# Index scores earlier, two feature tiles in the attention loop, query blocks in reverse order

## The chip, the cores and the metric

One core of one Trainium2 chip runs the whole program. The time is the device time of one execution in microseconds; the figure that counts is the median of the runs. The names in the profile are PE (TensorE matmuls), PEld (its weight loads), DVE (VectorE), ACT (ScalarE), POOL (GpSimd) and SP (SyncE, which issues most DMAs).

## The reference

The reference is one inference step of two decoder layers on 512 prompt tokens and 8 samples, width 1024. Each layer normalises x, multiplies it by one input projection, and feeds four token mixers from column groups of the result; their outputs go through one output projection, and a gated feed-forward part follows. The mixer that the change touches is A, sparse attention: 8 indexer heads score every earlier key, each query keeps the best 128 (64 for a sample), and 4 heads of 64 attend over the kept keys.

```python
def select_keys(qi, wi, ki, qpos, topk):
    s = jnp.einsum('bqhd,bsd->bqhs', qi, ki) * IDX_DIM ** -0.5
    score = jnp.einsum('bqhs,bqh->bqs', jax.nn.relu(s), wi * N_IDX_HEADS ** -0.5)
    score = jnp.where(kpos[None, None, :] <= qpos[None, :, None], score, -jnp.inf)
    _, idx = lax.top_k(score, topk)
    return idx, idx <= qpos[None, :, None]
```

B is a short gated convolution, C a convolution of 31 taps with a layer norm, D a state-space scan with its own convolution of 4 taps.

## The kernel before, in words

Every engine runs one program written out in order by hand; semaphores join them, and `past(layer, sem, value)` is the count to wait for in a layer. [...] All of float32 accuracy is made of three products: a value is split into a rounded part (`hi`, cast on ScalarE) and the rest (`lo`, a subtraction), and hi*hi, hi*lo and lo*hi are summed in PSUM.

A layer of the kernel has these stages up to the output projection:

1. **Token tiles.** The queries, keys, values and indexer columns are made with tokens on the partitions, in 15 tiles `(s, t)`: slab s of three (0 indexer, 1 queries and half the keys, 2 the other half and the values), and t of four blocks of 128 tokens and the samples (t = 4, `QT`). `slab_upper` on ScalarE and `slab_lower` split the weight slabs: slab 0 on VectorE (`first_slab_lower`, L1731), slabs 1 and 2 on GpSimd (L2527). Tiles of slab 0 for t < 4 are made together (L729 to L743), the others one after another (L745 to L770). ScalarE copies each out (`tok_ready`).
2. **Index scores.** After tile (1,0), TensorE waits for VectorE's rotary (`rope_done` 2), transposes the indexer queries and keys (`turn`, L767 to L769), and issues 24 index products (3 query blocks by 8 heads, `IDX`), four at a time at half tiles from (1,1) to (1,4) (`IDX_PLACES`). ScalarE rectifies each (`idx_rectified`), VectorE weights and adds it (L1823 to L1832), with four PSUM banks and two buffers in SBUF between them.
3. **Top-k.** VectorE alone: the mask of future keys, the rotary of the queries (L1837), then 16 rounds of the eight largest and their replacement over three blocks (L1840 to L1851). In round 4 it turns aside for the rotary of the keys and the samples (L1841 to L1844), whose end (`rope_done` 5) GpSimd waits for before it stores k and goes on with its subtractions.
4. **Feature tiles.** Meanwhile TensorE makes the remaining columns with features on the partitions, in 18 tiles of 48 products (`feature_products`, L774). SP loads a weight tile, ScalarE casts it (`tile_upper`), GpSimd subtracts (`tile_lower`), and ScalarE copies the result out (`feature_out`, which casts the weights of the tile after next first, L1335). Tiles 0 to 6 come first (`SPREAD_FROM` = 7), then 24 products between each of 8 samples' spread rows (L811 to L813), on which VectorE computes the samples' scores (L1860 to L1877): 11 tiles up to the loop (`LOOP_TILES`).
5. **The attention loop** (L931 on TensorE, L1410 on ScalarE, L2099 on VectorE) has 16 steps, one per query block and head, in `STEPS` order, block 0 first. Per step VectorE masks the logits (L2107), ScalarE takes the exponential, VectorE scales (L2120), TensorE transposes the probabilities (L965), ScalarE copies them, and TensorE multiplies by the values, for two heads at once (L954); logits are made in pairs (L924). A block b has (b + 1) * 128 keys, so the size of all of these goes with the block. Between them VectorE does the samples' attention, the gates and the convolution of D, and from step 11 the rows of the samples' states (`state_rows`, L2053, which waits for TensorE's `turn_state_rows`) and the states; TensorE does `STEP_PRODUCTS[j]` feature products twice in each of steps 0 to 10, and from step 12 the taps of the long convolution (`conv_c_group`, L912). Up to tile 11 two pairs of banks alternate (`tile_bank`); later tiles have one pair, so that tile i waits until tile i - 1 has been copied out (L780). `tiles_ending` tells ScalarE in which half step a tile ends.
6. Then the scan of D, the last two feature tiles and the output projection follow.

```python
SPREAD_FROM = 7
STEP_PRODUCTS = (14, 12, 13, 9, 13, 9, 13, 9, 13, 9, 9)
LOOP_TILES = SPREAD_FROM + NS * PER_SPREAD // PER_TILE
```

Of the kernel before, what the change touches and what calls it, by code (L numbers as in the profile page):

```python
# [22 lines left out]
F32 = mybir.dt.float32  # L23
# [94 lines left out]
def hybrid_decoder(nc, d, out):  # L118
# [24 lines left out]
    with ctx:  # L143
# [220 lines left out]
        first_lo = x8_turned  # L364
        per_layer[first_lo.num] = 2
        slab_hi, slab_lo = sem("slab_hi", 5), sem("slab_lo", 3)
# [77 lines left out]
        SPREAD_FROM = 7  # L444
# [3 lines left out]
        STEP_PRODUCTS = (14, 12, 13, 9, 13, 9, 13, 9, 13, 9, 9)  # L448
# [23 lines left out]
        STEPS = [(blk, h) for blk in range(QT) for h in range(HEADS)]  # L472
        IDX = [(blk, h) for blk in range(1, QT) for h in range(IH)]
        IDX_PLACES = [(1, 1, 1), (1, 2, 0), (1, 2, 1), (1, 3, 0), (1, 3, 1), (1, 4, 0)]
        IDX_AT = {place: range(4 * i, 4 * i + 4) for i, place in enumerate(IDX_PLACES)}

        def tok_bank(g):

            return 2 + g % 2 if g > QT else 7 if g == QT else 2 + g
# [20 lines left out]
        with nc.Block() as block:  # L500
# [126 lines left out]
            def _(pe):  # L627
# [23 lines left out]
                for layer in range(DEPTH):  # L651
# [58 lines left out]
                    g = 0  # L710
                    for s in range(N_TOK):
                        if s == 1:
# [16 lines left out]
                        if s == 0:  # L729
                            starts = [a for a, _, _, _ in tok_pieces[0]]  # L730
                            for k in range(KC):
                                pe.wait_ge(*past(layer, m_lo_ready, k + 1))
                                if k in starts:
                                    pe.wait_ge(*past(layer, first_lo, starts.index(k) + 2))
                                hi, lo = tok_k_of(tw_hi, 0, k), tok_k_of(tw_lo, 0, k)
                                for t in range(QT):
                                    to = bank(tok_bank(t))[:, 0:tok_w[0]]
                                    u_k, lo_k = u_hi[:, k, t * P:(t + 1) * P], m_lo[k][:, t * P:(t + 1) * P]
                                    pe.matmul(to, u_k, hi, start=(k == 0), stop=False)  # L739
                                    pe.matmul(to, u_k, lo, start=False, stop=False)  # L740
                                    last = pe.matmul(to, lo_k, hi, start=False, stop=(k == KC - 1))  # L741
                                    if k == KC - 1:
                                        last.then_inc(tok_summed, 1)  # L743
                            g = QT
                        for t in range(QT if s == 0 else 0, QT + 1):  # L745
                            m = P if t < QT else NS
                            to = bank(tok_bank(g))[0:m, 0:tok_w[s]]
                            if g > QT:
                                pe.wait_ge(*past(layer, tok_ready, g - 1))
                            for k in range(KC):  # L750
                                if s and t == 0 and k in [a for a, _, _, _ in tok_pieces[s]]:
                                    pe.wait_ge(*past(layer, slab_lo, sum(len(p) for p in tok_pieces[1:s]) +
                                               [a for a, _, _, _ in tok_pieces[s]].index(k) + 1))
                                u_k, lo_k = u_hi[:, k, t * P:t * P + m], m_lo[k][:, t * P:t * P + m]
# [4 lines left out]
                                if k == KC // 2 - 1:  # L759
                                    idx_products((s, t, 0))  # L760
# [170 lines left out]
                    for j in range(-1, len(STEPS) + 2):  # L931
# [13 lines left out]
                        if j >= 3 and j % 2:  # L945
                            blk, h = STEPS[j - 3]
                            pe.wait_ge(*past(layer, prob_t_ready, j - 1))
                            if h == 0 and blk >= 1:
                                pe.wait_ge(*past(layer, mixed_out, blk))
# [1683 lines left out]
```

## Time and profile before

| | us |
|---|---|
| Median of 3 runs | 1466.51 |
| Lowest, highest | 1465.22, 1470.06 |
| Profiled execution | 1465.05 |
| Its span, first to last instruction | 1463.3 |
| Busy PE, DVE, ACT, POOL | 1368.9, 1017.8, 652.4, 184.2 |
| Mean granted TensorE clock | 0.964 |

A window row gives the stretch in us from the start of the span, its length, the busy time of PE, PEld, DVE, ACT and POOL with the count of instructions, the granted TensorE clock (1.00 is 2.4 GHz, 0.50 is 1.2 GHz), the DMA share and GB/s. A timeline row gives start, duration, engine, line, operation, output and inputs by name, partitions and elements, and the count merged into the row; in square brackets stands how long the engine was idle before it and whose instruction released it. Durations of merged rows are those of the whole group.

### The profile page before, as it was taken

Reading aid. Unit: us, or ns where it says so; the run is one execution under the profiler, and the core shown is the slowest. Engines: PE = TensorE matmul, PEld = TensorE weight load, DVE = VectorE, ACT = ScalarE, POOL = GpSimd, SP = SyncE. Lnnn points to the kernel's source line nnn. Section 1 sums busy time; section 2 is a strip of 40 time slices with the busy share of each in tenths; the row PEclk is TensorE's granted clock in tenths of the full one; section 3 lists DMA queues with packets and bytes.
Section 4 is the critical chain, followed back from the end, with each engine's and each line's share of the span. In section 5 each row is a group of like instructions: output and inputs, shape, how many; then the busy total and the mean of one; then the engine's idle time right before and its main releaser. Section 6 shows DMA issues by size and latency. Waiting matters only on the chain.

```text
span 1463.3 us, 29326 instructions
## 1 busy us (share of the span) xinstructions
PE 1368.9 (94%) x11014; PEld 1267.0 (87%) x11014; DVE 1017.8 (70%) x2141; ACT 652.4 (45%) x1202; POOL 184.2 (13%) x132
## 2 busy tenths in 40 slices
PE   5999979997999999999879998899979999999997
PEld 5789865787999999999767997648979999999996
DVE  5489898744899999322366898987259999982223
ACT  4443335444556666322244422445344665653222
POOL 0334312021000000001030442121100000000000
PEclk9999989998999999999979999999989999999998
DMA  7443231221523333433254333212223233335321
GB/s 267 123 126 101 66 94 61 93 72 44 159 73 108 107 101 101 155 91 98 95 165 127 100 84 94 66 69 82 88 81 108 88 114 102 100 97 160 88 88 59
DMA packets 223892, 149.85 MB, mean 102 GB/s; under 512 B 13650, under 2 KB 218810, under 8 KB 222758
## 3 DMA queue, kind: packets, MB, share of 16 engines
q1 hardware_dynamic: 221174, 141.09, 32.4%
q0 software_dynamic: 2624, 7.48, 1.4%
q8 instruction: 63, 1.03, 0.3%
q14 instruction: 31, 0.25, 0.1%
HBM read 128.92 MB, written 16.03 MB: 99 GB/s over the span
## 4 chain that ended last, share of the span: by engine, by line
PE 80%; DVE 14%; ACT 3%; issue 2%; SPq 1%; DMA 0%; POOL 0%; DVEq 0%; ACTq 0%
PE PS L684 29%; PE PS L1149 24%; PE PS L785 11%; PE PS L756 2%; PE PS L757 2%; PE PS L758 2%; PE PS L912 1%; DVE side L2016 1%; DVE x L2281 1%; PE PS L663 1%; PE PS L700 1%; PE PS L739 1%; PE PS L740 1%; PE PS L741 1%; DVE arena L1768 1%
## 5 line engine op out<-in xcount | busy, mean ns | idle before, releaser
L1149 PE MATMUL PS<-b_hi,a_hi 128*128 128x260 f32 x1008 | 286.2, 284 | 3.0 <-DVE last_lo L2364 2.2
L1149 PE MATMUL PS<-b_lo,a_hi 128*128 128x260 f32 x1008 | 284.4, 282 | 0.0
L2169 DVE TENSOR_TENSOR w_lo<-ring,w_hi 128x640 fp32r<-128x640 f32 (+2 forms) x88 | 87.5, 995 | 242.4 <-ACT w_hi L1403 242.1
L1149 PEld LDWEIGHTS PS<-b_hi,a_hi 128*128 128x128 f32 x1008 | 189.9, 188 | 4.5 <-DVE last_lo L2364 2.7
L1149 PEld LDWEIGHTS PS<-b_lo,a_hi 128*128 128x128 f32 x1008 | 190.3, 189 | 0.0
L1403 ACT CAST w_hi<-ring 128x1024 fp32r<-128x1024 f32 (+2 forms) x92 | 80.1, 871 | 234.3 <-PE PS L684 234.3
L785 PE MATMUL PS<-u_hi,w_hi 128*128 128x260 f32 x576 | 123.4, 296 | 13.6 <-ACT hid L1345 13.6
L684 PE MATMUL PS<-hid_hi,w_lo 128*128 128x260 f32 x656 | 132.3, 283 | 0.0
L684 PE MATMUL PS<-hid_hi,w_hi 128*128 128x260 f32 x656 | 132.1, 283 | 0.0
L684 PE MATMUL PS<-hid_lo,w_hi 128*128 128x260 f32 x656 | 131.9, 283 | 0.0
L1149 PE MATMUL PS<-b_hi,s_lo 128*128 128x260 f32 x432 | 122.1, 283 | 0.0
L1149 PE MATMUL PS<-b_hi,raw_lo 128*128 128x260 f32 x432 | 122.0, 282 | 0.0
L785 PE MATMUL PS<-m_lo,w_hi 128*128 128x260 f32 x576 | 121.2, 290 | 0.0
L785 PE MATMUL PS<-u_hi,w_lo 128*128 128x260 f32 x576 | 121.2, 291 | 0.0
L2524 POOL TENSOR_TENSOR w_lo<-ring,w_hi 128x1024 fp32r<-128x1024 f32 x36 | 86.7, 2408 | 267.7 <-ACT w_hi L1291 267.7
L785 PEld LDWEIGHTS PS<-u_hi,w_hi 128*128 128x128 f32 x576 | 92.2, 195 | 20.5 <-ACT hid L1345 15.0
L2594 POOL TENSOR_TENSOR side<-side 128x520 f32<-128x520 f32 x12 | 15.7, 1307 | 710.2 <-ACT u L1683 710.2
L684 PEld LDWEIGHTS PS<-hid_hi,w_lo 128*128 128x128 f32 x656 | 101.1, 189 | 0.0
L684 PEld LDWEIGHTS PS<-hid_hi,w_hi 128*128 128x128 f32 x656 | 101.1, 189 | 0.0
L684 PEld LDWEIGHTS PS<-hid_lo,w_hi 128*128 128x128 f32 x656 | 101.0, 189 | 0.0
L1575 ACT CAST a_hi<-ring 128x512 fp32r<-128x512 f32 x144 | 89.5, 621 | 16.5 <-PE PS L1149 16.2
L785 PEld LDWEIGHTS PS<-m_lo,w_hi 128*128 128x128 f32 x576 | 91.9, 194 | 2.8 <-issue 2.8
(401 smaller groups left out, 3329.1 us busy)
## 6 DMA issues: line engine op xcount, KB each, us to landing
ring<-in_ffn_gate SPq DMA_DIRECT2D x44, 512.0 KB, 3.7
ring<-in_ffn_up SPq DMA_DIRECT2D x44, 512.0 KB, 3.7
ring<-in_w_in SPq DMA_DIRECT2D x36, 512.0 KB, 3.6
ring<-in_ffn_down SPq DMA_DIRECT2D x32, 384.0 KB, 3.4
ring<-in_ffn_down SPq DMA_DIRECT2D x32, 320.0 KB, 3.0
x_store<-x SPq DMA_DIRECT2D x4, 2080.0 KB
x<-x_store SPq DMA_DIRECT2D x4, 2080.0 KB, 8.3
ring<-in_w_out SPq DMA_DIRECT2D x16, 512.0 KB, 4.2
```

The costliest lines, as they stand in the source:

```text
L663: last = pe.matmul(to[:, g // 2, (g % 2) * QUARTER:(g % 2 + 1) * QUARTER], ident[:, 32 * g:32 * g + 1].broadcast_to([P, P]), rstd[:, :], s ...
L684: ins = pe.matmul(to[:, h, :], w[:, k - base, :], a[k][:, h * HALF:(h + 1) * HALF], start=(begin and w is whi and a is a_hi), stop=(end an ...
L756: pe.matmul(to, u_k, hi, start=(k == 0), stop=False)
L757: pe.matmul(to, u_k, lo, start=False, stop=False)
L758: last = pe.matmul(to, lo_k, hi, start=False, stop=(k == KC - 1))
L785: last = pe.matmul(bank(tile_bank(i) + h)[:, 0:HALF], w[i % 2][:, k, :], t[:, h * HALF:(h + 1) * HALF], start=(k == 0 and a == 0), stop=(k ...
L1149: ins = pe.matmul(bank(ACC[up][to])[:, 0:HALF], w[:, k, :], b[:, k, :], start=(start and k == 0 and w is whi and b is bhi), stop=(k == KC ...
L1403: act.copy(w_hi[part % 2][:, 0:n, :], raw[part % 4][:, 0:n, :]).then_inc(part_hi, 1)
L1575: act.copy(a_hi[hi_block(q, at)][:, :, :], source if q not in (S1, S2, S4) else source[:, :, :])\
L2169: dve.tensor_tensor(w_lo[part % 2][:, 0:n, :], raw[part % 4][:, 0:n, :], w_hi[part % 2][:, 0:n, :].bitcast(F32), ALU.subtract).then_inc(pa ...
L2524: pool.tensor_tensor(w_lo[f % 2][:, :, :], raw[(f + 2) % 4], w_hi[f % 2][:, :, :].bitcast(F32), ALU.subtract).then_inc(tile_lo, 1)
L2594: pool.tensor_tensor(squares[:, 0, :], squares[:, 0, :], squares[:, m, :], ALU.add).then_inc(added, 1)
```

## The change

Five things are altered. (1) The tiles go in the order `TOK_TILES`: (1,0) before the sample tile (0,4), the transposes of the indexer within (0,4), and the 24 index products three at a time, from the end of (0,4) to the third quarter of (1,2). (2) Slabs 1 and 2 are cast by ScalarE in one go right after u, and their subtraction goes from GpSimd to VectorE, right after the normalisation. (3) The addition of the dt bias is moved behind the queries' rotary, and the rotary of keys and samples from round 4 of top-k to round 8. (4) `SPREAD_FROM` is 5, so 9 tiles are done before the loop and 7 in it, with more products per step. (5) `STEPS` runs through the query blocks from the last (512 keys) to the first.

```diff
-        slab_hi, slab_lo = sem("slab_hi", 5), sem("slab_lo", 3)
+        slab_hi, slab_lo = sem("slab_hi", 5), sem("slab_lo", 5)
...
-        SPREAD_FROM = 7
+        SPREAD_FROM = 5
...
-        STEP_PRODUCTS = (14, 12, 13, 9, 13, 9, 13, 9, 13, 9, 9)
+        STEP_PRODUCTS = (18, 16, 17, 13, 17, 14, 17, 14, 17, 13, 12)
...
-        STEPS = [(blk, h) for blk in range(QT) for h in range(HEADS)]
+        STEPS = [(blk, h) for blk in reversed(range(QT)) for h in range(HEADS)]
         IDX = [(blk, h) for blk in range(1, QT) for h in range(IH)]
-        IDX_PLACES = [(1, 1, 1), (1, 2, 0), (1, 2, 1), (1, 3, 0), (1, 3, 1), (1, 4, 0)]
-        IDX_AT = {place: range(4 * i, 4 * i + 4) for i, place in enumerate(IDX_PLACES)}
+        TOK_TILES = [(0, t) for t in range(QT)] + [(1, 0), (0, QT)] + [(1, t) for t in range(1, QT + 1)] + [(2, t) for t in range(QT + 1)]
+        TURN_QI = (0, QT, 0)
+        IDX_PLACES = [(0, QT, 3)] + [(1, 1, q) for q in range(4)] + [(1, 2, q) for q in range(3)]
+        IDX_AT = {place: range(3 * i, 3 * i + 3) for i, place in enumerate(IDX_PLACES)}
...
 # TensorE, per tile of TOK_TILES from the fifth on
+                        pe.wait_ge(*past(layer, tok_ready, g - 1 if g > QT + 1 else g - QT + 1))
+                        for k in range(KC):
...
+                            if k % 2:
+                                if (s, t, k // 2) == TURN_QI:
+                                    pe.wait_ge(*past(layer, rope_done, 2))
+                                    pe.wait_ge(*past(layer, tok_ready, QT))
+                                    turn(tok_qi, 0, bank(4))
+                                    turn(tok_qi, 1, bank(5))
+                                    turn(ki_four, 0, bank(6))
+                                idx_products((s, t, k // 2))
...
-                            if h == 0 and blk >= 1:
-                                pe.wait_ge(*past(layer, mixed_out, blk))
+                            if h == 0 and blk < QT - 1:
+                                pe.wait_ge(*past(layer, mixed_out, QT - 1 - blk))
...
 # ScalarE, after the casts of u
-                    slab_upper(1, 0)
+                    for s in range(1, N_TOK):
+                        for i in range(len(tok_pieces[s])):
+                            slab_upper(s, i)
...
 # VectorE, after take_states is defined and before the indexer's rotary
+                    for s in range(1, N_TOK):
+                        for i in range(len(tok_pieces[s])):
+                            slab_lower(s, i)
...
                     rope_tiles(tok_q, HEADS, HD, 16, tab, (QT + 1) + QT).then_inc(rope_done, 1)
                     dve.wait_ge(*past(layer, rope_done, 3))
+                    dve.wait_ge(*past(layer, tok_ready, QT + 2))
+                    dve.wait_ge(*past(layer, states_ready, 4))
+                    step(dve.tensor_tensor(per_head(dt_v), per_head(dt_v), head_all[:, 0:1, :].broadcast_to(blocks), ALU.add))
+                    settle()
+                    dve.scalar_tensor_tensor(dt_e, dt_v, -1.0, dt_v, ALU.mult, ALU.min).then_inc(dt_low, 1)
 
                     for r in range(TOPK_PROMPT // 8):
-                        if r == 4:
+                        if r == 8:
                             rope_tiles(tok_k, HEADS, HD, 16, tab, 2 * (QT + 1) + QT).then_inc(rope_done, 1)
...
 # GpSimd
-                    for s in range(1, N_TOK):
-                        for i in range(len(tok_pieces[s])):
-                            slab_lower(s, i)
                     tile_lower(0)
                     tile_lower(1)
...
-                        if f == 6:
+                        if f == SPREAD_FROM:
                             pool.wait_ge(*past(layer, rows_hi_ready, 3))
```

(The lines with `#` in the diff are headings for the reader.) ScalarE's loop over the tiles follows the same order, and `slab_lower` is the same subtraction with `dve` in place of `pool`.

## Rows read from the trace of the kernel before

**Rows 1.** The page: busy shares, then the chain's shares by engine.

```profile
PE 1368.9 (94%) x11014; PEld 1267.0 (87%) x11014; DVE 1017.8 (70%) x2141; ACT 652.4 (45%) x1202; POOL 184.2 (13%) x132
...
PE 80%; DVE 14%; ACT 3%; issue 2%; SPq 1%; DMA 0%; POOL 0%; DVEq 0%; ACTq 0%
```

**Rows 2.** Windows by stage: span, busy of PE, PEld, DVE, ACT, POOL, clock, DMA.

```profile
44.00:80.00 36.00, 35.38 (x222) 27.86 (x221) 23.88 (x48) 16.27 (x44) 4.86 (x2) 1.00 0.45 122
80.00:140.00 60.00, 60.00 (x456) 57.64 (x454) 54.77 (x156) 24.74 (x52) 26.14 (x19) 1.00 0.41 116
140.00:170.00 30.00, 30.00 (x226) 27.59 (x226) 27.07 (x63) 6.00 (x9) 9.60 (x4) 1.00 0.28 74
170.00:233.00 63.00, 50.67 (x389) 41.65 (x389) 58.90 (x176) 24.20 (x54) 14.71 (x14) 0.91 0.29 76
233.00:268.00 35.00, 33.68 (x257) 15.98 (x257) 28.83 (x109) 17.40 (x36) 6.42 (x10) 0.91 0.21 72
```

**Rows 3.** Timeline of VectorE to top-k: start, us, line, operation, [idle <-releaser].

```profile
20.18 2.73 DVE L1734 TENSOR_TENSOR tw_lo<-tw_raw,tw_hi 128x1200 fp32r<-128x1200 f32 x2
...
44.86 4.29 DVE L1768 TENSOR_TENSOR arena<-arena,cst 128x256 f32<-128x256 f32 x1 [11.55 <-ACT arena L1307]
...
57.93 0.35 DVE L1829 TENSOR_SCALAR arena<-arena 128x256 f32<-128x256 f32 x1 [5.39 <-ACT arena L1279]
...
79.64 1.48 DVE L1847 MAX8 chunk_best<-arena 128x8 f32<-128x256 f32 x3
...
97.78 0.28 DVE L1768 TENSOR_TENSOR arena<-tok,cst 8x128 f32<-8x128 f32 x1 [2.87 <-ACT tok L1304]
```

**Rows 4.** Timeline of GpSimd, slab subtraction.

```profile
41.91 6.95 POOL L2530 TENSOR_TENSOR tw_lo<-tw_raw,tw_hi 128x1152 fp32r<-128x1152 f32 x2 [0.37 <-ACT tw_hi L1260]
```

**Rows 5.** Timeline of TensorE, first matmul of token tile (1,0).

```profile
46.08 0.44 PE L756 MATMUL PS<-tw_hi,u_hi 128*128 128x384 f32 x1
```

**Rows 6.** The chain in order of time: start, us, line.

```profile
110.47 28.84 PE PS L785 x240
...
169.51 0.47 PE PS L924 x4
```

**Rows 7.** Timeline of VectorE: a sample, the loop's first mask, two convolutions.

```profile
162.70 0.69 DVE L1864 TENSOR_TENSOR side<-side,PS 128x512 f32<-128x512 f32 x1 [0.69 <-PE PS L799]
...
169.96 0.29 DVE L2107 CUSTOM_DVE_ANT_0 arena<-PS,cst 128x128 f32<-128x128 f32 x1 [0.42 <-PE PS L924]
...
211.73 2.32 DVE L2016 SCALAR_TENSOR_TENSOR side<-hid,par,side 128x511 f32<-128x511 f32 x3
...
215.88 4.33 DVE L2016 SCALAR_TENSOR_TENSOR side<-hid,par,side 128x511 f32<-128x511 f32 x3
```

**Rows 8.** Timeline of ScalarE: a tile's end in the loop.

```profile
204.65 1.03 ACT L1291 CAST w_hi<-ring 128x1024 fp32r<-128x1024 f32 x1
205.58 0.59 ACT L1345 ACTIVATE hid<-PS 128x520 f32<-128x520 f32 x1
```

**Rows 9.** Waits of TensorE, both layers: total us, times, longest.

```profile
PE PS L785 <- ACT hid L1345: 13.6, 6, 3.8
```

**Rows 10.** Timeline of TensorE: mixes, logits, transposes.

```profile
184.69 0.44 PE L954 MATMUL PS<-arena 128*64 128x128 f32 x4
...
245.29 1.13 PE L924 MATMUL PS<-arena 64*128 64x512 f32 x4
...
254.78 1.09 PE L954 MATMUL PS<-arena 128*64 128x128 f32 x16
255.80 0.66 PE L965 MATMUL PS<-cst,arena 128*128 128x128 f32 x4
```

**Rows 11.** Windows of 4 us in the loop, same columns.

```profile
184.00:188.00 4.00, 2.02 (x16) 1.19 (x14) 3.73 (x16) 0.76 (x3) 0.00 (x0) 0.97 0.41 98
188.00:192.00 4.00, 2.53 (x11) 2.02 (x9) 3.73 (x15) 1.38 (x2) 0.25 (x1) 0.50 0.42 99
...
204.00:208.00 4.00, 1.77 (x15) 1.77 (x16) 3.86 (x8) 2.20 (x5) 2.24 (x1) 1.00 0.39 116
```

More of the change, by code:

```diff
@@ L728, in _ @@
                               .then_inc(states_turned, 1)
[L729 to L754, printed above, removed]
-                                hi, lo = tok_k_of(tw_hi, s, k), tok_k_of(tw_lo, s, k)
-                                pe.matmul(to, u_k, hi, start=(k == 0), stop=False)
-                                pe.matmul(to, u_k, lo, start=False, stop=False)
-                                last = pe.matmul(to, lo_k, hi, start=False, stop=(k == KC - 1))
-                                if k == KC // 2 - 1:
-                                    idx_products((s, t, 0))
-                            last.then_inc(tok_summed, 1)
-                            g += 1
-                            if s == 1 and t == 0:
-                                pe.wait_ge(*past(layer, rope_done, 2))
-                                pe.wait_ge(*past(layer, tok_ready, QT + 1))
-                                turn(tok_qi, 0, bank(4))
-                                turn(tok_qi, 1, bank(5))
-                                turn(ki_four, 0, bank(6))
-                            idx_products((s, t, 1))
@@ new lines, in _ @@
+                        m = P if t < QT else NS
+                        to = bank(tok_bank(g))[0:m, 0:tok_w[s]]
+                        pe.wait_ge(*past(layer, tok_ready, g - 1 if g > QT + 1 else g - QT + 1))
+                        for k in range(KC):
+                            if t == 0 and k in [a for a, _, _, _ in tok_pieces[s]]:
+                                pe.wait_ge(*past(layer, slab_lo, sum(len(p) for p in tok_pieces[:s]) +
+                                           [a for a, _, _, _ in tok_pieces[s]].index(k) + 1))
+                            u_k, lo_k = u_hi[:, k, t * P:t * P + m], m_lo[k][:, t * P:t * P + m]
+                            hi, lo = tok_k_of(tw_hi, s, k), tok_k_of(tw_lo, s, k)
+                            pe.matmul(to, u_k, hi, start=(k == 0), stop=False)
+                            pe.matmul(to, u_k, lo, start=False, stop=False)
+                            last = pe.matmul(to, lo_k, hi, start=False, stop=(k == KC - 1))
+                            if k == KC - 1:
+                                last.then_inc(tok_summed, 1)
+                            if k % 2:
[6 more added lines that the diff above has]
+                                idx_products((s, t, k // 2))
@@ L1815, in _ @@
                     blocks = [P, QT + 1, HEADS]
-                    dve.wait_ge(*past(layer, tok_ready, QT + 1))
-                    dve.wait_ge(*past(layer, states_ready, 4))
-                    step(dve.tensor_tensor(per_head(dt_v), per_head(dt_v), head_all[:, 0:1, :].broadcast_to(blocks), ALU.add))
-                    settle()
-                    dve.scalar_tensor_tensor(dt_e, dt_v, -1.0, dt_v, ALU.mult, ALU.min).then_inc(dt_low, 1)
                     for n, (blk, h) in enumerate(IDX):
```

94 lines of the change are left out of this document (48 added, 46 removed).

## The prediction

> **What bounds the kernel now.** I read the busy shares first, then the chain of waits: TensorE is busy 94% of the span and carries 80% of the chain, VectorE 14% [rows 1]. The share does not say where time can be won, so the next view was the windows by stage. Both layers run the same stages 720 us apart, so I work in layer 0 and double. From 80 to 170 us TensorE never idles (60.00 of 60, 30.00 of 30), and VectorE is nearly full beside it (54.77, 27.07). From 170 to 233, the attention loop, TensorE is busy only 50.67 of 63 with a mean granted clock of 0.91, and VectorE 58.90 of 63: VectorE sets the pace there. From 233 to 268, the end of the loop, TensorE is busy 33.68 of 35 [rows 2]. So there are 12.3 us of TensorE idle time per layer in one stage, and work can be put into it only if that stage begins earlier and VectorE has nothing more to do in it.
>
> **The change part by part** (layer 0, us of the profiled execution).
>
> *Index scores.* VectorE idles 11.55 before its first rotary product, and that product (0.42 for the same shape in the queries' rotary) takes 4.29, because GpSimd runs its slab subtraction from 41.91 for 6.95 [rows 3, 4]. After the change these subtractions (two of 3072 columns altogether; two of 1200 took 2.73, so about 3.5 each, 7 in all) lie on VectorE in that idle time, done near 41.6, before token tiles 0 to 3 are out at 42.0. They cost nothing; without that cover they would cost up to 7. The indexer rotary, moved up by the absence of GpSimd, ends near 44.4. TensorE does the (1,0) tile (24 matmuls of 384 columns, the first at 46.08, the last out near 50.5 [rows 5]) before the sample tile now, so it reaches the transposes near 48 without the wait it has (0.62 before), and the first index score is on VectorE at about 52.6, against 57.93. The 24 additions themselves are 15.7 busy in an interval of 19.8; products come three at a time at quarter tiles, and I let them end at 68.7. Next late is a new thing: the rotary of the queries needs token tile (1,3), which TensorE ends near 71.4 (67.2 for (1,2) and its index products, plus 4.2) and ScalarE copies out by 72.1. Top-k begins at 72.1 + 1.3 (rotary) + 0.45 (the moved dt additions) = 73.9, against 79.64: 5.7 earlier [rows 3]. In top-k the two waits for token tiles go, the longer of 2.87 [rows 3], since round 8 falls near 99.7 and the last token tile is out at 97. VectorE then reaches the samples, 13 us earlier, near 130.6.
>
> *Two tiles out of the stage before.* Nothing of that is time yet, because TensorE is full there. What moves the loop's start is that 96 feature products leave: 240 took 28.84, so 0.120 each and 11.6 together [rows 6]. Add the 0.6 of the transposes' wait, take off 0.3 for two more breaks between tile and index products and 0.4 for GpSimd, whose DMA issues now wait for a rotary that ends near 104 instead of 102 and have its third subtraction behind them, for which TensorE waits at 110. The first mask of the loop comes at 158.7 instead of 169.96 [rows 7]: 11.3 earlier. VectorE reaches the samples' stage at 130.6, TensorE spreads its first row near 127.8, and VectorE, which waited 0.69 for TensorE before each of the last samples [rows 7], needs that much less for each of eight and has caught up by the end: TensorE sets 158.0 for its first logits. GpSimd's low rows are ready at 127.0, 0.8 before they are asked for.
>
> *The loop up to step 11.* TensorE had 50.7 busy. It gets 11.6 of products, and 4.2 of attention work that the reversed order brings forward (below). Of its half-clock time (9% of 63 is 5.7 lost, some 4.6 of it in busy time) I assume that it goes as the idle time goes. Work: 50.7 + 11.6 + 4.2 - 4.6 = 61.9. Then the waits. In the loop a tile has one pair of banks; the next may start only when ScalarE has cast a weight tile (1.03) and copied the result (0.59), 1.7 with the signals [rows 8]. Before, three tiles per layer meet this: 13.6 in 6 waits, the longest 3.8 [rows 9]. Now five do (tiles 11 to 15). ScalarE works in order, so such a copy also stands behind the exponential of its step, and this behind VectorE's mask. Laid out by steps, four cost 1.7 and tile 12, which ends two products into step 6, waits for the mask of step 6 and costs 4.1: 10.9. With 0.7 for waits on probabilities that is 73.5, and the rows for the sample states come at 158.7 + 73.5 = 232.2 against 233.4. VectorE needs less: 58.9, 1.6 for longer masks and scalings, and two more GpSimd subtractions in the loop, each of which can hold a convolution step (three took 2.32 free and 4.33 beside one [rows 7]), so 2 each: 64.5, with its waits about 68. So the bound changes hands: of 11.3 only 1.2 is left here.
>
> *The end of the loop.* Blocks of 128 keys replace those of 512. A pair of logits falls from 1.13 to 0.47, twice: 1.3 [rows 6, 10]. Three pairs of mixes go from 12, 16 and 16 matmuls to 8, 4 and 4 (16 took 1.09, 4 took 0.44): 1.5. Transposes: 13 fewer, at 0.11 each by what four of them (0.66) take over one (0.33): 1.4 [rows 10]. Sum 4.2, on an engine that is busy 33.7 of 35 here, beside a VectorE that also has 0.5 less per step; ScalarE's convolution activations (5.8 with table loads) fit. After the loop the same work follows in the same order: 0.
>
> *Sum.* 1.2 + 4.2 = 5.4 per layer, 10.8 in all. The profiled execution took 1465.05 (span 1463.3 and 1.75 around it): 1454.3. The median of the runs is 1.46 above it, so I say 1455.7.
>
> *A rule against the trace.* TensorE's granted clock fell to 0.50 in 188 to 192, after 2.02 busy of 4, but stayed at 1.00 from 204 to 208 with only 1.77 busy [rows 11]. The Trainium skill (TensorE: Matmul & The Clock Gate, "Part 1: The HAM clock gate") says that the array drops to 1.2 GHz when it has been idle and comes back only after sustained activity. The trace agrees once and not the second time. By that rule five stalls instead of three would give more slow stretches, and that is the third rival below.
>
> **The rivals.** *VectorE stays the bound.* If ScalarE is never behind and TensorE's waits overlap, the loop takes 68 + 1.8 for the turn to the sample rows, 69.8: 4.9 + 4.2 = 9.1 per layer, 1448. For it: 58.90 of 63; against: single banks. *ScalarE behind at every tile end.* Each of the other four waits costs 3.0 instead of 1.7 (between 1.7 and the longest 3.8): 5.2 per layer eat the gain, 1466. For it: the mean now is 2.3; against: the loop has less VectorE lead to wait for. *The clock, which makes it slower.* A mean of 0.91 over 63 us is 11.3 us at the half level, 5.7 lost [rows 2]. While TensorE had slack this cost little; in the fuller loop it is paid. If the five waits bring a second stretch as long as the first, the 4.6 that I took off stay and 5.7 come on top: 10.3 per layer, minus 5.4 is +4.9, twice, 1476. It decides from 10.8 us of half clock per layer in the loop, which is what is there now. For it: more tile ends; against: far less idle time between them. That the change does nothing at all is excluded for the loop's start, which TensorE alone sets.
>
> **How the numbers follow.** Forecast 0.50 (its own range 1451 to 1460), VectorE the bound 0.15, ScalarE behind 0.15, clock 0.20. The range of 1446 to 1475 reaches to the first rival's far side and to nearly all of the third. A measurement tells about 0.3%, 4.4 us, from no change. Faster by more: nine tenths of the 0.50 and the 0.15 of the first rival, some 0.61; within it the second rival and the forecast's lower edge, 0.20; slower the most of the clock's share, 0.19.
>
> **What would show it.** First index addition near 52.6, a wait of about 3 for the queries' rotary, top-k from 73.9; the loop's first mask at 158.7; the windows of the loop with TensorE at 84% or more; ten waits of the feature products for ScalarE instead of six, about 22 in sum; the sample rows near 232; the end of the taps 5 earlier. Wrong would be a loop start that moved by less than 9, a granted clock below 0.9 in the loop, or a VectorE wait for decode results of several us that I have not put in.

## The result, and the profile after

The changed kernel takes 1479.44 us (median of 4 runs, 1478.91 to 1480.69), the kernel before 1466.51 (1465.22 to 1470.06). The ratio is 1.0086 with a 95% interval of 1.0073 to 1.0099: slower by 13 us, where 1455.7 was forecast. The profiled execution has a span of 1478.9 us against 1463.3; it is the slowest of its four, so the stages below add up to some 16 us and not to 13.

Busy times and the chain's shares, from the page after, answer to [rows 1]:

```profile
PE 1380.1 (93%) x11014; PEld 1266.3 (86%) x11014; DVE 1018.8 (69%) x2147; ACT 652.4 (44%) x1202; POOL 157.9 (11%) x126
...
PE 76%; DVE 17%; ACT 3%; issue 2%; POOL 1%; DMA 1%; SPq 0%; DVEq 0%; ACTq 0%
```

The number of matmuls is the same (11014), and yet TensorE is busy 11 us longer. Work did not grow, so each piece took longer on average. The windows by stage say where; columns are as in [rows 2], the clock is the third number from the end:

```profile
44.00:80.00 36.00, 36.00 (x217) 26.23 (x216) 22.80 (x55) 15.65 (x38) 0.00 (x0) 1.00 0.41 111
80.00:140.00 60.00, 59.79 (x441) 56.61 (x440) 58.52 (x164) 24.14 (x51) 25.34 (x19) 1.00 0.41 116
...
160.80:239.40 78.60, 66.45 (x533) 56.42 (x535) 60.93 (x176) 29.39 (x58) 20.26 (x17) 0.93 0.28 74
239.40:276.30 36.90, 32.84 (x194) 11.99 (x194) 24.85 (x105) 13.02 (x34) 5.98 (x10) 0.72 0.14 46
```

The same two stages of the kernel before, cut at its own events (first mask, sample-state rows, end of the taps):

```profile
170.00:233.40 63.40, 51.07 (x393) 42.04 (x395) 59.30 (x177) 24.48 (x55) 15.11 (x15) 0.91 0.29 75
233.40:266.20 32.80, 31.48 (x240) 13.79 (x236) 28.14 (x108) 15.83 (x34) 6.02 (x9) 0.92 0.16 54
```

Up to 160.8 us all is well: the loop begins 9.2 us earlier. It then lasts 15.2 us longer (78.6 against 63.4), and the stretch behind it, which I call the tail, 4.1 longer (36.9 against 32.8). Together layer 0 is 10.1 us longer; layer 1 adds 5.8. A mean clock of 0.93 over 78.6 us is 5.5 us lost (before: 0.91, 5.7), and 0.72 over 36.9 is 10.3 us lost (before: 0.92, 2.6). These figures count idle time as well as busy time, so they are upper bounds of what the clock cost. So the loop kept its loss, and the tail, with 46 matmuls fewer, took a new one of 7.7 us.

Windows of 4 us show where the clock falls, twice in the loop and once in the tail (a fourth fall, to 0.68, is at 264 us):

```profile
196.00:200.00 4.00, 2.19 (x18) 1.98 (x18) 3.52 (x15) 2.39 (x6) 0.74 (x1) 1.00 0.42 98
200.00:204.00 4.00, 4.00 (x23) 4.00 (x23) 3.96 (x4) 0.48 (x1) 2.19 (x1) 0.57 0.45 105
...
208.00:212.00 4.00, 2.31 (x19) 1.44 (x14) 1.08 (x5) 2.52 (x5) 1.01 (x1) 1.00 0.37 83
212.00:216.00 4.00, 4.00 (x35) 3.80 (x34) 2.41 (x6) 0.00 (x0) 1.36 (x1) 1.00 0.68 198
216.00:220.00 4.00, 2.33 (x20) 2.12 (x18) 3.82 (x10) 3.88 (x7) 0.00 (x0) 1.00 0.27 80
220.00:224.00 4.00, 2.49 (x11) 2.45 (x11) 3.93 (x4) 1.45 (x3) 2.85 (x1) 0.63 0.00 0
...
240.00:244.00 4.00, 2.70 (x16) 1.66 (x16) 3.84 (x11) 0.75 (x3) 1.25 (x2) 0.69 0.79 259
244.00:248.00 4.00, 2.22 (x12) 0.69 (x14) 3.86 (x10) 1.64 (x7) 0.00 (x0) 0.50 0.38 138
248.00:252.00 4.00, 4.00 (x16) 1.35 (x8) 0.77 (x6) 0.99 (x4) 3.05 (x6) 0.50 0.05 12
252.00:256.00 4.00, 4.00 (x22) 1.81 (x25) 3.19 (x16) 2.10 (x4) 0.00 (x0) 0.50 0.04 9
```

Each fall stands in or behind a stretch in which TensorE had idle time, and full work at the lower level (0.50 is 1.2 GHz) follows it. Not every such stretch brings a fall: 2.31 of 4 busy at 208 us was followed by 1.00. A group of 24 tap products takes 1.8 times as long there, and VectorE, which needs its results from the same queue, waits. First TensorE's taps (start, us, line), after:

```profile
254.50 4.73 PE L905 MATMUL PS<-arena,side 128*32 128x504 f32 x24
260.54 2.66 PE L905 MATMUL PS<-arena,side 128*32 128x492 f32 x24
```

and VectorE in the same kernel, from the first index addition to the sample states:

```profile
53.19 0.35 DVE L1817 TENSOR_SCALAR arena<-arena 128x256 f32<-128x256 f32 x1 [7.11 <-ACT arena L1274]
...
73.94 0.43 DVE L1759 TENSOR_TENSOR arena<-arena,cst 128x256 f32<-128x256 f32 x1 [1.95 <-ACT arena L1307]
...
75.58 1.47 DVE L1840 MAX8 chunk_best<-arena 128x8 f32<-128x256 f32 x3
...
160.77 0.69 DVE L2100 CUSTOM_DVE_ANT_0 arena<-PS,arena 128x512 f32<-128x512 f32 x1 [1.05 <-PE PS L917]
...
213.49 0.23 DVE L1997 COPY side<-PS 128x64 f32<-128x64 f32 x1 [2.97 <-PE PS L829]
...
239.42 0.17 DVE L2050 COPY small<-PS 128x16 f32<-128x16 f32 x1 [3.73 <-PE PS L869]
...
252.52 1.12 DVE L2068 TENSOR_SCALAR side<-PS,side 128x128 f32<-128x128 f32 x4 [3.68 <-PE PS L880]
```

The first four of these rows answer to [rows 3, 7]: index scores, rotary, top-k and first mask come earlier. The last three are waits for TensorE: in the loop VectorE no longer sets the pace. The waits of TensorE for tile ends, both layers, answer to [rows 9]:

```profile
PE PS L778 <- ACT hid L1336: 20.2, 10, 3.2
```

### The profile page after: what moved, and what is told of

Read it like the earlier page. It is cut to its first block, busy times and chain, and to the rows that moved or that the text cites. A ratio compares the mean times of both kernels' runs of the same rounds, so it can differ in the third digit from the quotient of the medians.

```text
span 1478.9 us, 29324 instructions
## 1 busy us (share of the span) xinstructions
PE 1380.1 (93%) x11014; PEld 1266.3 (86%) x11014; DVE 1018.8 (69%) x2147; ACT 652.4 (44%) x1202; POOL 157.9 (11%) x126
## 4 chain that ended last, share of the span: by engine, by line
PE 76%; DVE 17%; ACT 3%; issue 2%; POOL 1%; DMA 1%; SPq 0%; DVEq 0%; ACTq 0%
PE PS L684 28%; PE PS L1142 24%; PE PS L778 9%; PE PS L905 2%; DVE arena L1844 2%; DVE chunk_best L1840 2%; PE PS L751 1%; DVE x L2274 1%; PE PS L700 1%; PE PS L753 1%; PE PS L752 1%; PE PS L663 1%; PE PS L719 1%; PE PS L720 1%; PE PS L721 1%
## 5 line engine op out<-in xcount | busy, mean ns | idle before, releaser
L778 PE MATMUL PS<-u_hi,w_hi 128*128 128x260 f32 x576 | 123.7, 295 | 20.6 <-ACT hid L1336 20.2
L778 PEld LDWEIGHTS PS<-u_hi,w_lo 128*128 128x128 f32 x576 | 90.4, 191 | 3.5 <-issue 3.5
```

Source lines behind the costliest of these rows:

```text
L778: last = pe.matmul(bank(tile_bank(i) + h)[:, 0:HALF], w[i % 2][:, k, :], t[:, h * HALF:(h + 1) * HALF], start=(k == 0 and a == 0), stop=(k ...
```

## The experiments

My first theory: the moved tiles made TensorE the bound of the loop, so that its half clock is now paid (that far it is the third rival), and the *reversed order* empties TensorE at steps 11 to 13 and so costs the tail its clock. "Before" below is always the kernel before on the same chip; a ratio is to its runs. Times of stages are from layer 0 of the profiled executions.

### 1. Forward order again

```diff
-STEPS = [(blk, h) for blk in reversed(range(QT)) for h in range(HEADS)]
+STEPS = [(blk, h) for blk in range(QT) for h in range(HEADS)]
```

> The change with its query blocks in the forward order again (index scores early and the two feature tiles in the loop are kept). Theory: the reversed order empties TensorE at steps 11 to 13, its clock falls to 1.2 GHz for some 18 us and the taps run there (10.3 us lost to the clock behind the state rows of layer 0, 2.6 in the kernel before). Forward, state rows to last taps take about 33 us instead of 36.9 (granted clock there back near 0.92), and the loop to the state rows about 74 instead of 78.6; in all some 4 to 5 us per layer less than the change: about 1470. Rival: the order does not matter, the two moved tiles cost the time; then the tail stays near 37 us and the time is 1477 or more.

Measured 1480.72, ratio 1.0080 (1.0066 to 1.0094): no better than the change. The tail is 38.1 us, not 33. Its windows, loop and tail:

```profile
160.30:236.50 76.20, 63.53 (x487) 54.20 (x489) 58.24 (x176) 27.29 (x58) 19.22 (x16) 0.91 0.30 77
236.50:274.60 38.10, 33.82 (x242) 14.52 (x241) 28.21 (x108) 16.11 (x34) 6.27 (x10) 0.87 0.14 47
```

The half of my theory that blames the order falls. The clock is lost in loop and tail without it. The order is not without effect on the tail's clock, though: reversal alone (experiment 3) reads 0.84 there, the tiles in forward order 0.87, both together 0.72.

### 2. The two tiles undone

```diff
-SPREAD_FROM = 5
-STEP_PRODUCTS = (18, 16, 17, 13, 17, 14, 17, 14, 17, 13, 12)
+SPREAD_FROM = 7
+STEP_PRODUCTS = (14, 12, 13, 9, 13, 9, 13, 9, 13, 9, 9)
```

> The change with the two feature tiles taken out of the loop again (seven tiles before it, early index scores and reversed blocks kept). Theory: the loop is bound by VectorE again, 65 us to the state rows instead of 78.6, but it starts 10 to 12 us later; the tail keeps its half clock and its 36 to 37 us. The time is about 1477, close to the change. Rival: the moved tiles alone are the cause; then this is at or under the kernel before, 1468 or less.

Measured 1471.87, ratio 1.0024 (1.0013 to 1.0035). Neither theory had this: 3.5 to 4.2 us of the loss are left without the tiles (by the ratio and by the medians), and the tiles carry the rest, some 8 to 9. Loop 66.4, tail 31.9 with the clock at 0.84. Compared with this run, the tiles bring the first mask forward by 12.5 us (173.3 to 160.8) and cost 12.2 in the loop and 5.0 in the tail. Of the 12.5, 1.1 is no work of theirs: the matmuls of token tile (1,0), the same in both kernels, begin at 44.15 here and at 43.08 after the change. From there to the first mask the difference is 11.5, as the 11.6 of 96 products say.

### 3. Index scores alone, reversal alone, tiles alone

The first undoes tiles and order of the change, the other two make one edit each to the kernel before.

> Only the early index scores, with tiles and order as in the kernel before. Theory: the scores land some 4.5 us earlier, the loop begins when TensorE has made seven tiles and so at the same time or up to 1 us earlier; 1463 to 1467. Rival: a part of the loss is in the index scores (the wait for the rotary of the queries, the GpSimd subtractions now on VectorE): 1470 or more.

Measured 1472.44, ratio 1.0031 (1.0020 to 1.0042): its rival. Top-k begins 4.1 us earlier (75.5), and the first mask still comes 1.6 later (171.6). TensorE has no idle time to give there; from 41 to 98 us it spends 7.0 us on the 48 index products instead of 5.8, start to start. They are cut in eight groups between token products instead of six; experiment 8 shows that this is half of the difference.

> Only the reversed order of the query blocks, on the kernel before. With the early index scores the reversed order cost 2.4 to 2.7 us in each loop and 0.8 to 1.7 us ahead of it and gave 2.9 back in each tail. Theory (the order moves time from the tail into the loop and is worth nothing in sum, whatever the clock): loop about 66, tail 30 to 32, 1464 to 1470. Rival: the order costs the clock by itself, tail of 35 or more: 1473 or more.

Measured 1468.49, ratio 1.0006 (0.9996 to 1.0015), loop 66.1 (before 63.4), tail 31.4 (before 32.8): worth nothing in sum, as the theory said. The forecast had a gain of 4.2 us per layer from it in the tail; here the tail gives 1.5 and the loop takes 2.7.

> Only the two feature tiles moved into the loop, index scores and order as in the kernel before. The top-k still starts at 79.6 us, and the samples stage can't start before VectorE is through it, at about 138 us instead of 134. Theory: the first mask comes at 164 to 165 instead of 160.8, the loop stays TensorE-bound at 74 to 78 and the tail loses its clock: 1482 to 1488. Rival: the early index scores cost more than they bring (1472.4 alone): 1479 or less.

Measured 1496.77, ratio 1.0202 (1.0179 to 1.0225), worse than either. The first mask comes at 168.2, 1.8 earlier than before, not 5 as I had it. The samples begin at 142.2 there against 133.9 with the early scores: without them VectorE gets out of top-k 8.3 us later, and I put the missing advance of the first mask down to that. So the parts don't add: 5 (index scores) and 30 (tiles) make 13 together with the order. The early scores alone cost time; under the tiles they give 16 back (1480.72 with both and forward blocks, against 1496.77).

### 4. Wide products at step 12, to keep TensorE busy

```diff
 if j == 12:
+    pe.wait_ge(*past(layer, dec_out, 4))
+    keep_warm(3)     # matmul(bank(3), ones, cst[:, 0:512])
     turn_tails()
+    keep_warm(3)
```

> The change with six matrix products of 512 columns added per layer, three before and three behind the turning of the tail rows at step 12 of the loop, into a bank that nobody reads (1.3 us of TensorE at full clock, 2.6 at half). Theory: TensorE is no longer idle at steps 11 to 13, the granted clock of 241 to 259 us of layer 0 rises from 0.5 to near 1, and some 7 us of the 10.3 that the clock takes there come back: 1465 to 1470. Rival: the tail is a chain of waits and the clock only goes with it: the clock may rise, but the time stays at 1479 or above, by the added work.

Measured 1472.35, ratio 1.0031 (1.0021 to 1.0041): above the 1465 to 1470 of the theory, and 7 us under the change. I had mis-sized the products: six take 5.6 us, not 1.3. With 5.6 us of useless work *added* to TensorE, the tail got 4.8 us shorter, 32.1 instead of 36.9, and its clock went to 0.95:

```profile
239.50:271.60 32.10, 31.12 (x206) 12.16 (x206) 24.84 (x105) 13.01 (x34) 5.97 (x10) 0.95 0.16 53
```

### 5. Narrow products ahead of tile-end waits in the loop, and behind them

```diff
 if at == 0:
+    if i in (13, 14, 15):
+        keep_warm(12, bank(2 if i == 15 else 3)[:, 0:252])
     if i >= 2:
         pe.wait_ge(*past(layer, feat_ready, i - 1 if i <= LOOP_TILES + 1 else i))
     pe.wait_ge(*past(layer, tile_lo, i + 1))
```

Twelve products of 252 columns took 1.56 us. In the control the same lines stand behind the two waits.

> The change, with twelve narrow products of 252 columns (about 0.12 us each, 1.4 in all) put ahead of three of TensorE's five waits for ScalarE at tile ends in the loop, those of tiles 13, 14 and 15, into a bank that nobody reads. They fit into waits of 1.7 to 3.2 us. Theory: the 5.5 us that the half clock takes in the loop of layer 0 come back, first mask to sample-state rows falls from 78.6 to 73 to 75, and the time is 1469 to 1474, or less if the tail keeps its clock too. Rival: the loop is bound by the round trips to ScalarE and VectorE, the clock costs nothing beside them: the loop stays at 78 or more, the time at 1478 to 1482.

> The same 36 narrow products per layer as in the version with warm products ahead of three tile-end waits in the loop (1466.9), with the same operands and banks, but behind those waits instead of ahead of them, so that TensorE stands idle as in the change and works 1.4 us more each time. Theory (the clock fell because TensorE was idle, and what helped was the filled idle time): the half clock stays at 200 us and at 220 to 228 us, the loop grows by 4 us or more to 82 to 84 us, the time is 1486 to 1492. Rival (what helped was some other effect of the products, their place in the queue or more products in all): under 1476.

Ahead of the waits: 1466.93, ratio 0.9999 (0.9989 to 1.0010), 12 us less than the change and under the 1469 to 1474 of the theory. Behind them: 1486.90, ratio 1.0122 (1.0101 to 1.0144). The same 72 instructions, 20 us apart by the medians and 18 by the ratios. Ahead, they stand in time in which TensorE was idle, and the window that fell to 0.57 after the change keeps its clock:

```profile
196.00:200.00 4.00, 3.58 (x29) 3.38 (x30) 3.56 (x15) 2.46 (x6) 0.66 (x1) 1.00 0.43 100
200.00:204.00 4.00, 4.00 (x35) 4.00 (x35) 3.93 (x4) 0.48 (x1) 2.28 (x1) 1.00 0.44 102
```

The tail is 32.2 although nothing was put there; its clock reads 0.89. Why it fared better no run takes apart. Behind the waits, layer 0 held its loop clock too (0.98, where I expected it to fall) and was 80.0 long; its tail fell to 0.72, and layer 1 lost the clock in both. That part of my expectation was wrong, the total (1486 to 1492) right. Behind the waits the products' own time is exposed, 3 by 1.56 us, 9.4 in two layers; the change and 9.4 would be 1488.8, and 1486.9 was measured. So of the 20 us some 9 are the products themselves. The rest goes with the clock, above all in the tails, which read 0.72 and 0.73 behind the waits and 0.89 and 0.89 ahead of them. The same products help where they stand in idle time, and not where they don't. That the control held the clock of layer 0's loop all the same (0.98) is left open.

### 6. All places, on the change, on the forward order and on the kernel before

"All" is the three places above, 10 products ahead of `turn_state_rows` and 20 and 20 around `turn_tails`.

> The same three places, and the narrow products also ahead of the turning of the state rows (10) and on both sides of the turning of the tail rows (20 and 20). Theory: loop 73 to 75 and tail at or under 31, so some 9 us less than the change per layer: 1460 to 1466. Rival: what the loop gives back, the tail takes (the loop's gain only makes TensorE wait later): no better than the change with warm products at step 12 alone, 1472.

> The change with its blocks forward again and with all the warm products of the version that came to 1465.3 with reversed blocks. Theory: with the clock held, the order is worth what the smaller blocks save behind the state rows, 2 to 3 us per layer, less what they cost in the loop: 1465 to 1470. Rival: forward is as good or better once the clock is full, as it was without warm products: 1465 or less.

> The kernel before, with the narrow products ahead of the turning of the state rows (10) and around the turning of the tail rows (20 and 20), nothing else. Theory: the kernel before lost 2.6 us of clock behind the state rows, at most that comes back per layer, against 4.8 us of added products of which some 2 fall into waits: 1462 to 1468, no more than 3 us under the kernel before. Rival: warm products are worth 3 to 5 us per layer in any kernel of this kind (the gain seen in the change has nothing to do with the moved tiles): 1460 or less.

Measured 1465.25, ratio 0.9982 (0.9973 to 0.9991); 1466.80, 0.9992 (0.9983 to 1.0001); and 1467.36, 0.9992 (0.9984 to 1.0001). At this clock the order is not to be told apart: 75.8 and 31.7 us of loop and tail reversed, 73.7 and 34.3 forward, 107.5 and 108.0 in sum. The kernel before gains nothing from the 50 products of the tail, the only ones that it got; its loop still reads 0.95 and 0.92, so what products at its tile ends would bring was not run. The nearest to it is the run without tiles in experiment 8, whose loop reads 1.00 and which is no faster than the kernel before (1.0004). The loop of the first was expected at 73 to 75 and came to 75.8, because the clock still fell to 0.72 at 220 us, behind the wait of tile 15.

### 7. The change at full clock

The cut is against the first kernel of experiment 6.

```diff
-    if i in (13, 14, 15):
-        keep_warm(12, bank(2 if i == 15 else 3)[:, 0:252])
+    if i in (11, 13, 14, 15):
+        keep_warm(24 if i == 15 else 12, bank({11: 7, 15: 2}.get(i, 3))[:, 0:252])
```

> The change itself (two tiles in the loop, reversed blocks) with narrow products ahead of four of its five tile-end waits (tiles 11, 13, 14 with 12 each, tile 15 with 24, whose wait is 3.2 us), 10 ahead of the turning of the state rows, 20 and 20 around that of the tail rows. Theory: this is what the forecast of 1455.7 took for granted, full clock through the loop. Loop of layer 0 at 73 to 74 us (forecast 73.5), tail about 30 to 31 (forecast 28.7), first mask 161.5: 1460 to 1463. Rival: the second tile costs more than TensorE time, the loop stays at 75 to 76 with the clock full: 1465 as with three places.

Measured 1461.39, ratio 0.9957 (0.9944 to 0.9969), 18 us less than the change. Windows of its loop and tail:

```profile
161.20:235.50 74.30, 70.36 (x603) 61.08 (x605) 60.86 (x177) 29.50 (x59) 20.32 (x17) 1.00 0.30 79
235.50:265.70 30.20, 29.03 (x234) 14.49 (x232) 24.82 (x105) 13.00 (x34) 5.96 (x10) 1.00 0.17 56
```

With 110 useless products per layer, loop and tail of layer 0 are 104.5 us instead of 115.5 (layer 1: 105.6, its tail at 0.95, instead of 112.2). This is the forecast's own sum at the clock that it took for granted: 74.3 against 73.5, and 30.2 against 28.6 (32.8 less 4.2). The tail's 30.2 holds 40 of the added products, some 5 us, and so is not a measurement of the same work.

### 8. One tile instead of two, and the best version

```diff
-SPREAD_FROM = 5
-STEP_PRODUCTS = (18, 16, 17, 13, 17, 14, 17, 14, 17, 13, 12)
+SPREAD_FROM = 6
+STEP_PRODUCTS = (16, 14, 15, 11, 15, 12, 15, 11, 15, 11, 9)
```

(and tile 11 waits for the copy of tile 10, with which it now shares its banks).

> The change with one feature tile moved into the loop instead of two (six ahead of it, 288 products in it instead of 336, and one more wait for the eviction of the first of them). Theory: the loop's cost is TensorE time, a tile in the loop costs as much as it saved ahead of it (5.8 us each way) plus the clock that TensorE loses behind it; half of the two tiles' loss is left: about 1475, between 1471.9 (no tile moved) and 1479.4 (two). Rival: TensorE's idle time in the loop holds one tile but not two: 1468 or less.

> One feature tile in the loop instead of two, with twelve narrow products ahead of each of the five tile-end waits in it, 10 ahead of the turning of the state rows and 20 and 20 around the turning of the tail rows. Theory: without half clock the loop of layer 0 falls from 71.7 to about 68 and that of layer 1 from 69.2 to 68, the tail stays at 31.4: 1461 to 1465, the best so far. Rival: at full clock the loop is bound by VectorE and nothing comes back: 1468.

> Early index scores and reversed order, no tile moved, with the warm products of the run above. Theory: it differs from the one-tile version with warm products (1460.3) by the tile: that gained some 6 us ahead of the loop and cost under 3 in it as long as the clock is full. So here 1464 to 1469. Rival: the gain of the one-tile version is the clock alone, any version at full clock comes to it: 1462 or less.

One tile: 1468.03, ratio 1.0001 (0.9992 to 1.0009), which is the rival; my halving was too simple, because the clock's loss does not go by halves: the tail reads 0.84 with no tile moved and with one, 0.72 with two. With 12 narrow products ahead of all five tile ends (60) and the 50 of the tail: 1460.27, ratio 0.9946 (0.9933 to 0.9960). No tile, with 24 products in the loop and the 50 of the tail: 1467.58, ratio 1.0004 (0.9995 to 1.0013). The one-tile loop, layer 0 and layer 1:

```profile
167.50:235.10 67.60, 64.47 (x555) 55.19 (x557) 59.63 (x176) 28.17 (x56) 17.09 (x16) 1.00 0.31 79
```

```profile
884.20:951.80 67.60, 64.43 (x555) 55.15 (x557) 59.72 (x176) 28.21 (x56) 17.07 (x15) 1.00 0.30 79
```

At a steady clock the loops of both layers are alike to a tenth; after the change they were 78.6 and 77.0. At full clock, counted from the first product of token tile (1,0), each of the two tiles brings the first mask forward by 5.7 us (from 129.2 to 123.5 and 117.7). The first costs 3.4 in the loop and 0.3 in the tail, the second 6.6 in the loop, and is worth nothing. (The versions differ in added products too: 74, 110 and 110 per layer.)

The index products put back into six groups of four, as early as in the change, and then also fewer products in the tail (8 and 8 instead of 20 and 20) and 22 instead of 12 ahead of the wait of tile 12:

```diff
-IDX_PLACES = [(0, QT, 3)] + [(1, 1, q) for q in range(4)] + [(1, 2, q) for q in range(3)]
+IDX_PLACES = [(0, QT, 3), (1, 1, 0), (1, 1, 2), (1, 2, 0), (1, 2, 2), (1, 3, 0)]
```

> The one-tile version with warm products (1460.3), its index products in six places of four heads instead of eight places of three, as coarse as in the kernel before, though as early. Theory: the early index scores cost TensorE 1.2 us more between 41 and 98 us for their finer interleaving (index products 7.0 us of TensorE's time instead of 5.8); half of that or more comes back per layer: first mask at 166.5 to 167 instead of 167.5, 1458 to 1460. Rival: it is the waits of those products for ScalarE and VectorE, which coarser groups make no shorter: 1460 to 1462.

> The best version (one tile, six places of four heads, warm products; 1459.7) with 8 and 8 instead of 20 and 20 narrow products around the turning of the tail rows and 22 instead of 12 ahead of the wait of tile 12 (2.85 us without them). Theory: 24 products fewer on a chain that TensorE bounds behind the state rows are 2.9 us per layer less if the clock stays full with 8: tail 28 to 30, 1455 to 1459. Rival: 8 are too few, the clock falls again at about 240 us: 1460 to 1464.

1459.68, ratio 0.9948 (0.9935 to 0.9961), and 1460.11, ratio 0.9934 (0.9920 to 0.9948). In the trace the coarser groups bring the first mask from 167.5 to 166.6 (0.9) and the span from 1458.7 to 1455.4, but that execution is the fastest of its five and the other the slowest; the medians of the three versions can't be told apart. The index products take 6.4 us in six early groups, against 7.0 in eight early ones and 5.8 in the six later ones of the kernel before. So 0.6 of the 1.2 goes with the number of groups; the other 0.6 stays, and nearly all of it lies in the second group, which takes 1.35 where before it took 0.64. In the lean one the clock fell once more in layer 0, to 0.66 at 256 to 260 us, and its tail was 31.2 instead of 30.2 (29.5 instead of 29.9 in layer 1): neither theory is decided. All three beat both kernels: they are 0.5 to 0.7% under the kernel before and 1.3% under the change.

### 9. What is left of the index scores' cost

> Only the early index scores (tiles and order as before; 1472.4 without warm products, 5 us over the kernel before), with twelve narrow products ahead of the tile-end waits of tiles 14 and 15, 10 ahead of the turning of the state rows, 20 and 20 around that of the tail rows. Theory: of the 5 us some 1.6 per layer are TensorE time in the index scores (first mask at 171.6 instead of 170.0) and stay, the rest is half clock behind the state rows and returns: tail 33 to 34 instead of 34.8, 1468 to 1471. Rival: all of it is clock: 1465 or less; or none is: 1472 to 1476.

Measured 1471.10, ratio 1.0032 (1.0021 to 1.0044), with a profiled span 2.8 us shorter than without the products, and the ratio the same. Its loop still had two stretches at half clock (0.50 at 192 us, 0.57 at 208), for which I had no free bank earlier. Without products, the early scores cost 1.6 us of first mask in each layer against the kernel before, and 1.4 to 1.9 of tail (34.8 against 32.8). With the products at step 11 and 12 in both kernels, both tails read 1.00, and they are 34.1 against 33.8 (layer 1: 33.4 and 33.4): that part goes with the clock. The first mask is then 1.2 later in layer 0 and 0.5 in layer 1. Where the rest of the 4 us between the medians (1471.10 and 1467.36) lies stays open; the two profiled executions have the same span, 1467.4.

## Why the prediction was wrong, point by point

**Index scores: right, one term too small.** First addition at 53.2 (forecast 52.6). The wait for the queries' rotary is 1.95 (about 3), top-k begins at 75.6 instead of 73.9. What ends last there is not the additions, late as they are (71.3, forecast 68.7), but the copy of token tile (1,3), from which the queries come: 73.9 instead of 72.1, behind TensorE. The GpSimd subtractions on VectorE cost nothing, as said.

**The loop's first mask: 160.8, forecast 158.7.** The 11.6 us of two tiles did come off TensorE (11.5 in experiment 2). What was mis-sized is the move of the index products: I took 0.3 us for two more breaks, it is 1.2, half of it by the finer groups. The reversed order begins with a pair of logits over 512 keys, 1.13 against 0.47, which I had not counted: 0.6 to 0.7. The remaining 0.5 is open; 0.2 of it is in my sum, whose terms give 11.5 and not the 11.3 that I wrote.

**The loop: the first step that failed.** The prediction said "Of its half-clock time (9% of 63 is 5.7 lost, some 4.6 of it in busy time) I assume that it goes as the idle time goes." It did not: 5.5 us stayed. TensorE was busy 66.45 us where I had 61.9, which is the 4.6 that I took off; 73.5 + 4.6 is 78.1, and 78.6 was measured. The waits for ScalarE were right in sum: 20.2 in 10 (about 22). The long one is that of tile 15 (3.18), not of tile 12 (1.69, forecast 4.1). The bound did change hands. With the clock held, the loop is 74.3. I had the rule and a row for it [rows 11] and set it aside since one window of two spoke against it; the idle time went from 12.3 to 12.2 us (78.6 less 66.45), not down at all. Four rows of TensorE's timeline in the loop of the kernel before show why:

```profile
187.12 0.33 PE L965 MATMUL PS<-cst,arena 128*128 128x128 f32 x1 [1.99 <-DVE arena L2120]
192.22 0.80 PE L785 MATMUL PS<-u_hi,w_hi 128*128 128x260 f32 x2 [1.69 <-ACT hid L1345]
206.23 0.51 PE L785 MATMUL PS<-u_hi,w_hi 128*128 128x260 f32 x2 [2.98 <-ACT hid L1345]
216.96 0.51 PE L785 MATMUL PS<-u_hi,w_hi 128*128 128x260 f32 x2 [1.69 <-ACT hid L1345]
```

Of its 12.3 us idle only 3.3 were waits for VectorE; 6.4 were the three tile ends, and 2.5 two other waits for ScalarE's copies. So I had misread this idle time as slack that VectorE left. After the change 0.9 is VectorE's, 10.1 are five tile ends and 1.2 another copy. More products can fill a wait for VectorE, but they add tile ends. The prediction held the contradiction itself: 10.9 us of waits stood next to an assumption that idle time goes.

**The tail, the second step that failed: "4.2 less" became 4.1 more.** The smaller blocks give 1.4 to 2.9 (reversal alone; with the early scores), and 2.6 in the pair of experiment 6, not 4.2. I priced the tail at the clock of the kernel before, without a reason. The clock took 10.3 us instead of 2.6: 7.7, half of the 15.5 below. That TensorE would idle at the end of the loop (2.70 and 2.22 of 4 us, waiting for tails and probabilities) was not in the prediction. The attention work that I moved forward out of this stretch may have kept it busier; but the forward order with the tiles loses there too (38.1 us, 0.71 busy of 4 at 240 us), so the order is not the whole of it. Why the tiles cost the tail its clock no run takes apart.

**The sum of layer 0**: 2.1 (first mask) + 5.1 (loop) + 8.3 (tail, 36.9 against 28.6) = 15.5; the forecast of 5.4 us gained becomes 10.1 lost, as measured.

**The rivals.** VectorE as the bound: wrong, it waits for TensorE 3.73, 3.68 and 2.97 us in single waits (the kind of wait that I had named as a sign against the forecast). ScalarE behind at every tile end: wrong, 1.7 was the usual wait. The clock, with 0.20, was the mechanism; it gave 1476, 3.4 us short. It had a second stretch of half clock in the loop on top of the first; there were two short ones with the old sum, and the new loss came in the tail. That its figure came near is in part luck. Its "decides from 10.8 us of half clock" was in effect met: 11.0 in the loop. The range ended at 1475 and so left out the very figure of that rival. (The chances have a slip too: nine tenths of 0.65 is 0.585, not 0.61.) Experiments 4, 5 and 7 show this cause by filling idle time; that early scores and the tiles only pay together came as a fourth thing that no case held.

## What to carry to other kernels

When work is moved into an engine's idle time, ask of each wait who ends it and what it turns into: here 3.3 of 12.3 us were waits for the engine that I took for the bound, and 12.2 us stayed idle when 11.6 us of work had been put in. Price a stretch in which TensorE has idle time at both clock levels, and take the slow one as the forecast if the trace of before already shows it and the idle time stays. And test the clock with products that stand *ahead* of a wait, in a bank nobody uses, with the same ones behind it as a control.

## What the runs showed of the hardware that I had not expected

Useless work made the kernel faster: 110 narrow products per layer, 14 us of TensorE in each, took 18 us off 1479.4. The Trainium skill (TensorE: Matmul & The Clock Gate, "Part 1: The HAM clock gate") describes the low level as the default, released by activity. The runs agree with that: with the waits filled, the loops of both layers read 1.00 (experiment 7); with products behind the waits (experiment 5) the loops read 0.98 and 0.95 and the tails 0.72 and 0.73.

The lower level outlasts the idle time ahead of it: from 248 to 256 us TensorE was busy 4.00 of 4 in two windows and still at 0.50. It also hits layers of the same program unevenly: 10.3 us lost in the tail of layer 0 after the change, 8.4 in layer 1 (0.76 over 35.2), while at a steady clock the two loops agree to 0.1.

Fine interleaving has a price of its own: 48 index products took 7.0 us of TensorE's time in eight early groups and 6.4 in six.
